# Norms of 512 tokens in a two-layer diffusion trunk: one tile of squares to sum in place of two, a chunk later, and the root's table loaded ahead

## What is computed

```python
def rmsnorm(x, w):
    xf = x.astype(jnp.float32)
    y = xf * lax.rsqrt(jnp.mean(xf * xf, axis=-1, keepdims=True) + EPS)
    return (y * w.astype(jnp.float32)).astype(x.dtype)

def modulate(h, shift, scale):
    return h * (1 + scale) + shift

x = x + 0.5 * mod[:, 2] * swiglu(modulate(rmsnorm(x, norm_w[0]), mod[:, 0], mod[:, 1]), ffn1_wi, ffn1_wo)
h = modulate(rmsnorm(x, norm_w[1]), mod[:, 3], mod[:, 4])
```

## Time and profile before

| | us |
|---|---|
| three runs | 1838.77, 1846.31, 1848.38; median 1846.31 |
| profiled execution, its own time | 1840.37 |
| its span, first to last instruction | 1838.2 |
| TensorE matmuls busy | 1821.0 |
| VectorE busy | 1120.6 |
| ScalarE busy | 694.2 |
| GpSimd busy | 99.3 |

### The profile page before, as it was taken

One profiled execution on the slowest core, in us unless ns is written; L12 is line 12 of the kernel. 1 busy time (PEld: TensorE's weight loads), 2 busy tenths in 40 slices (PEclk: granted clock), 3 DMA queues, 4 the chain that ended last, 5 costly groups with the idle time before them and its releaser, 6 DMA issues.

```text
span 1838.2 us, 26302 instructions
## 1 busy us (share of the span) xinstructions
PE 1821.0 (99%) x10125; PEld 1545.6 (84%) x10125; DVE 1120.6 (61%) x1506; ACT 694.2 (38%) x1093; POOL 99.3 (5%) x174
## 2 busy tenths in 40 slices
PE   8999999999999999999999999999999999999998
PEld 6788888888777789888888888888888889999998
DVE  5777736656554366877737558777322487676554
ACT  3433332144334324433332144333322365556553
POOL 0110001010000001000001010000000100000000
PEclk9999999999999999999999999999999999999999
DMA  9666526433222223666526435665232344446653
GB/s 335 216 186 189 159 99 224 146 77 93 80 81 69 88 84 127 183 189 190 159 92 229 148 115 172 180 196 162 92 103 91 73 146 138 149 147 197 194 195 114
DMA packets 187893, 271.49 MB, mean 148 GB/s; under 512 B 25388, under 2 KB 154908, under 8 KB 187804
## 3 DMA queue, kind: packets, MB, share of 16 engines
q1 hardware_dynamic: 168912, 202.74, 35.2%
q0 software_dynamic: 18432, 67.12, 11.8%
q10 hardware_dynamic: 460, 0.39, 0.1%
HBM read 269.16 MB, written 1.05 MB: 147 GB/s over the span
## 4 chain that ended last, share of the span: by engine, by line
PE 94%; DVE 2%; ACT 2%; issue 1%; DMA 0%; POOL 0%; SPq 0%; ACTq 0%; DVEq 0%
PE ps L573 23%; PE ps L574 23%; PE ps L575 23%; PE turned L573 2%; PE turned L575 2%; PE turned L574 2%; PE scored L573 2%; PE scored L575 2%; PE scored L574 2%; PE ps L630 2%; PE ps L632 2%; PE ps L642 2%; PE turned L943 1%; PE scored L912 1%; PE turned L926 1%; PE scored L604 1%
## 5 line engine op out<-in xcount | busy, mean ns | idle before, releaser
L1338 DVE TENSOR_TENSOR wL<-raw,wH 128x1024 fp32r<-128x1024 f32 x364 | 443.3, 1222 | 448.3 <-ACT wH L1054 448.0
L573 PE MATMUL ps<-hH,wH 128*128 128x512 f32 (+1 forms) x1832 | 652.8, 356 | 2.0 <-ACT T L1166 1.4
L574 PE MATMUL ps<-hL,wH 128*128 128x512 f32 (+1 forms) x1832 | 646.3, 353 | 0.0
L575 PE MATMUL ps<-hH,wL 128*128 128x512 f32 (+1 forms) x1832 | 646.1, 353 | 0.0
L1054 ACT ACTIVATE wH<-raw 128x1024 fp32r<-128x1024 f32 x364 | 383.3, 1057 | 667.2 <-PE ps L575 662.2
L573 PEld LDWEIGHTS ps<-hH,wH 128*128 128x128 f32 x1832 | 344.8, 188 | 69.8 <-issue 21.4
L575 PEld LDWEIGHTS ps<-hH,wL 128*128 128x128 f32 x1832 | 344.8, 188 | 48.2
L574 PEld LDWEIGHTS ps<-hL,wH 128*128 128x128 f32 x1832 | 344.9, 188 | 46.6
L573 PE MATMUL ps<-GH,wH 128*128 (+2 forms) x376 | 131.5, 350 | 0.0
L575 PE MATMUL ps<-GH,wL 128*128 (+2 forms) x376 | 131.2, 349 | 0.0
L574 PE MATMUL ps<-GL,wH 128*128 (+2 forms) x376 | 131.2, 349 | 0.0
(11 more groups left out here) (235 smaller groups left out, 2152.5 us busy)
## 6 DMA issues: line engine op xcount, KB each, us to landing
raw<-in_ffn_wi SPq DMA_DIRECT2D x176, 512.0 KB, 3.7
raw<-in_ffn_wo SPq DMA_DIRECT2D x88, 512.0 KB, 3.3
raw<-in_w_in SPq DMA_DIRECT2D x60, 512.0 KB, 3.9
adaC<-in_w_ada POOLq DMA_DIRECT2D x48, 512.0 KB, 4.5
adaW<-in_w_ada POOLq DMA_DIRECT2D x32, 512.0 KB, 4.6
adaA<-in_w_ada POOLq DMA_DIRECT2D x24, 512.0 KB, 4.0
adaB<-in_w_ada POOLq DMA_DIRECT2D x24, 512.0 KB, 4.6
raw<-in_w_out SPq DMA_DIRECT2D x16, 512.0 KB, 3.3
```

Source lines behind the costliest of these rows:

```text
L573: mm(dst, wa, ra, start=start, stop=False, **kw)
L574: mm(dst, wa, rb, start=False, stop=False, **kw)
L575: return mm(dst, wb, ra, start=False, stop=stop, **kw)
L1338: tt(wL[:, s, :], raw[:, s, :], wH[:, s, :].bitcast(F32), ALU.subtract).then_inc(lo_done, 1)
```

## The change

In the norms v = 1 to 4, GpSimd gets a fifth add for each half, of the tile with squares 6+7 into the tile with all the others, behind VectorE's add of 6+7. TensorE sums that one tile. The first half's sum moves from behind chunk 2 to behind chunk 3 and its spread from behind chunk 5 to behind chunk 6; the second half's from within chunk 1 to within chunk 2 and from within chunk 2 to within chunk 3. ScalarE's small activation that asks for the root's table stands ahead of the squares in norms 1 to 4 too.

```diff
-            return (0, 6) if beneath(v) else (0, 4, 6)
+            return (0,) if beneath(v) else (0, 4, 6)
...
-            each = [2 if q == 0 else 4 if beneath(q) else 3 for q in range(v + 1)]
+            each = [2 if q == 0 else 5 if beneath(q) else 3 for q in range(v + 1)]
...
-                    for i, (m, k) in enumerate(((0, 1), (2, 3), (0, 2)) + (((0, 4),) if beneath(v) else ())):
+                    for i, (m, k) in enumerate(((0, 1), (2, 3), (0, 2)) + (((0, 4), (0, 6)) if beneath(v) else ())):
...
-                            pool.wait_ge(sq_four, four_count(v, hf) + 3)
-                            pool.wait_ge(sq_pair, 2 * q + 1)
+                            pool.wait_ge(sq_four, four_count(v, hf) + i)
+                            pool.wait_ge(sq_pair, 2 * q + i - 2)
...
-                        if hf == 1 and at == 2:
+                        if hf == 1 and at == 3:
                             mean_squares(v, 0)
-                        if hf == 1 and at == 5:
+                        if hf == 1 and at == 6:
                             spread_roots(v, 0)
...
-                        pe.wait_ge(sq_four, four_count(v, hf) + (4 if beneath(v) else 3))
+                        pe.wait_ge(sq_four, four_count(v, hf) + (5 if beneath(v) else 3))
...
-                                  start=(m == 0 and tb == 0), stop=(m == 6), skip_group_check=True)
+                                  start=(m == 0 and tb == 0), stop=(m == sum_tiles(v)[-1]), skip_group_check=True)
...
-                return {(0, 1, "within"): lambda: mean_squares(v, 1), (0, 2, "within"): lambda: spread_roots(v, 1)}
+                return {(0, 2, "within"): lambda: mean_squares(v, 1), (0, 3, "within"): lambda: spread_roots(v, 1)}
...
                 if v > 0:
-                    if nh == 1:
-                        av(stat[:, 0, 0:1], epsT[:], ACT.Sqrt)
+                    av(stat[:, 0, 0:1], epsT[:], ACT.Sqrt)
```

## The result

| | before | after |
|---|---|---|
| median of 12 runs, us | 1838.65 | 1844.73 |
| lowest and highest | 1836.69, 1848.38 | 1842.92, 1853.31 |
| profiled execution, its span | 1838.2 | 1842.5 |

The ratio is 1.0031, with a 95% interval of 1.0021 to 1.0042: the change costs about 5.7 us, with bounds of 3.9 and 7.7. The forecast of the cost was +5.2 us. The forecast time of 1848.5 was 3.8 us too high, and the measured one lies in the range. All runs here are compared with runs of the kernel before on the same chip: e1 to e4 ran on one chip, e5 to e8 on another.

A forecast was written before the change was run, and what follows sets the result against it. TensorE, busy 1821.0 of 1838.2 us, was taken as the bound. Norms 1 to 4 cost 1.1 + 1.5 + 1.1 + 1.5 = +5.2 us, put on the mean 1843.5 for a forecast of 1848.5, range 1841 to 1856.

The forecast's parts named there:

- The prize: TensorE, norms 1 to 4: one tile less per sum saves 2.9 us, the first spread's lost wait 0.8; 3.7 in all.
- The table: ScalarE, norms 1 to 4: the root's 1.28 us table load, put ahead of the squares, falls in idle time, costing nothing.
- Rival C: At the root: the table does not last, a second 1.28 us load follows; +1 to +6 us on the forecast, chance 0.03.
- The sum of the first half: Norm 1: TensorE, ready at 398.65, waits 0.18 us for GpSimd's added add; the sum starts at 398.83.
- The first half's chain: Norm 1, spread to hH to opening: spread 0.33 us later, TensorE waits 0.68, opening at 403.43, 0.27 later than before.
- The second half: Norm 1: waits of 0.45 and 0.7 us for low parts of chunks 1 and 3; VectorE's diagonal 1.53 us later.
- Norms 2 and 4: VectorE's 1.53 us delay comes through whole, by the wait for hH in norm 2 and VectorE's list in 4; +1.5 each.
- norms 1 and 3: The wait for chunk 3's low part costs +1.1 us each; the modulation's sums that follow cover the rest.
- Rivals A and B: Norms 1 to 4: A, new waits all covered, -3.7 us, chance 0.12; B, clock halves, +15 us, chance 0.08.
- rival B: Norms 1 to 4: new waits let TensorE's clock fall to half, as after norm 5; +15 us or 1859, chance 0.08.

The follow-up runs named there:

- e1: Kernel before with only the root's table loaded ahead of the squares in norms 1 to 4: 1.22 us less over the norms, ratio 1.0002.
- e4: Changed kernel with the first half's spread back behind chunk 5 instead of 6: +2.74 us over norms 1 to 4 against before, ratio 1.0054.
- e5: Changed kernel with VectorE's low parts of weight piece and chunk 3 ahead of the second half's inverse root: +2.88 us over norms 1 to 4, ratio 1.0014.
- e8: Kernel before with twelve filling matmuls instead of six behind the spread of norm 5: ratio 0.9994, -0.01 us over norms 1 to 4.
- e3: Kernel before with the table ahead and the late sum and spread places, two tiles summed, no fifth add: +7.51 us over the norms, ratio 1.0055.
- e6: Changed kernel with both VectorE's list reordered and the first half's spread back behind chunk 5: +0.05 us over norms 1 to 4, ratio 0.9996.
- e7: Kernel before with the table ahead and VectorE's low part of the fourth weight piece one step later: -1.99 us over the norms, ratio 0.9977.
- e2: Changed kernel with sums and spreads back in their old places; one tile, fifth add and table ahead stay: +3.51 us over the norms, ratio 1.0028.

## Why the prediction was right

**The prize.** Right: 16 matmuls less (32 records), and the first spread's wait of 0.21 was gone, by the table (e1). The price of a tile was taken too low. I took the 0.36 between the starts of the two tiles. Where nothing waits, the matmuls on the two sides of the sum are 0.93 apart before (405.44 to 406.37) and 0.49 after, so a tile is worth 0.44; in the first half the wait for GpSimd eats it (see e3).

**The table.** Right: six loads ahead, none at the root's line, the load hidden in ScalarE's idle time. Rival C is out.

**The sum of the first half.** Predicted for norm 1 at 398.83 with a wait of 0.18; measured 399.00 with 0.19 (all measured times of this section are moved by the 1.72). TensorE was ready at 398.65, as predicted, so the wait recorded as 0.19 moved the sum by 0.35.

**The first half's chain.** Spread predicted at 401.52 and measured at 401.68, hH 402.77 and 402.84, opening 403.43 and 403.49, waiting 0.50 by the record and 0.68 by the sum.

**The second half.** hL matmuls of chunk 1 at 406.28 and 406.33, the sum at 407.72 and 407.86, the diagonal at 408.85 and 408.92, the hL matmuls of chunk 3 at 410.92 and 410.98. That what is queued behind the inverse root on VectorE carries the cost is shown by e5. The waits of L642 are recorded as 0.22 and 0.64; by the distances from start to start they cost 0.48 and 0.73, against the 0.45 and 0.7 of the sum.

**Norms 2 and 4.** Both wait at the second half's first matmul, and norm 4's two old waits are as long as before (0.69 and 1.26), since VectorE's whole list is late. They cost +1.56 and +1.58 against +1.5 each. The prediction says that norm 2 waits at this matmul in the kernel before already. The list of waits has none there, and the timeline leaves some 0.1 us for one: the four hL matmuls ahead take 0.59 from start to start (729.10 to 729.69), where those at 404.12 took 0.48.

```profile
729.10 0.64 PE L642 MATMUL ps<-hL,wH 128*128 128x256 f32 x4
729.69 0.35 PE L630 MATMUL ps<-hH,wH 128*128 128x256 f32 x1
```

**What was off.** Each of norms 1 and 3 was taken 0.15 too cheap and the total by 0.45 us. Of each 0.15, 0.1 is this: four hL matmuls that start from a wait cost 0.67 us (409.26 to 409.93), where I took their start alone to move; without a wait the same step took 0.57 (409.83 to 410.40). The level was off by 3.8 us. I put the 5.2 on the mean of four times (1843.5), which makes 1848.7 and not the 1848.5 written, but the median of before over 12 runs is 1838.65: two of the four times were of the upper group described below. The sum against the profiled execution's own 1840.37 gives 1845.6, within 0.9 us of the median measured. That the ratio of the runs gives 5.7 us, so near to the 5.65 of the traces, is partly luck: its interval is 3.9 to 7.7.

**Rivals A and B.** No chain was quicker than read. The granted clock was 1.00 in norm 1 (395 to 415 us) and in norm 4 (1462 to 1482), with TensorE busy for 18.5 and 16.4 of 20 us: waits of this size did not lower it. The row that rival B rests on does not show what the prediction says of it. From 1646.50 to 1648.00 TensorE is busy all the time, with filling matmuls of 128 columns. The 2-column matmuls and the waits lie ahead, from 1641.66 to 1644.67, and the clock fell there (it is 0.72 of full speed from 1643 to 1644 and 0.50 from 1644 to 1650). Nor does this stage always lower it. Here are the same 6.4 us around the spread of norm 5, first of before, then of e1: equally busy, once at half the clock and once at the full one.

```profile
1643.60:1650.00 6.40, 5.33 (x23) 0.50 0.28 86
```

```profile
1640.73:1647.13 6.40, 5.33 (x43) 1.00 0.28 86
```

## What to carry to other kernels

Before a step is moved later in one engine's list to hide a wait, follow the chain behind it: here the wait for GpSimd went from 0.9 us to 0.2 or nothing, and in norms 1 and 3 waits of 0.50, 0.22 and 0.64 us came back further on. A wait of an in-order engine delays all that is queued behind it, so work that is ready belongs ahead of it (e5 won 2.8 us with three lines in another order). And an edit of a tenth of a percent is read from the distance between two marks in the traces, which repeated within 0.04 us here, not from the whole time.

## What the runs showed of the hardware

**Two paces of the same matmuls at full clock.** Behind norm 5, from 1660 to 1820 us, TensorE works on matmuls of 256 columns, with one pause of 0.6 us. Two profiled executions, first of before, then of e4 (length, TensorE's busy time and matmuls, granted clock, DMA share, GB/s):

```profile
1660.00:1820.00 160.00, 159.38 (x1406) 1.00 0.59 190
```

```profile
1660.00:1820.00 160.00, 159.39 (x1355) 1.00 0.60 188
```

One does 1406 matmuls, the other 1355: 0.1133 against 0.1177 us from start to start, steady over the whole stretch. From the pause to the sum of norm 6 it is 166.86 us in before and 173.16 in e4:

```profile
1663.61 0.38 PE L573 MATMUL ps<-hH,wH 128*128 128x256 f32 x1 [0.62 <-ACT T L1147]
...
1830.47 0.58 PE L754 MATMUL scored<-cst,T 128*128 128x2 f32 x4 [0.23 <-DVE X L1424]
```

```profile
1666.02 0.38 PE L573 MATMUL ps<-hH,wH 128*128 128x256 f32 x1 [0.61 <-ACT T L1146]
...
1839.18 0.58 PE L754 MATMUL scored<-cst,T 128*128 128x2 f32 x4
```

The ten profiled executions have only these two lengths: 166.83 to 166.86 us in six, 173.16 to 173.17 in four, 6.3 us apart. Before, after, e1, e3, e6 and e7 ran it at the faster pace in their profiled execution, e2, e4, e5 and e8 at the slower. In e6 the 0.1177 shows earlier, from 1618 us to the end of the output projection, and is gone behind norm 5. It fits the two groups in the times of one kernel: of before, 17 of 25 runs beside e1 to e4 lie at 1836.7 to 1840.1 and the others at 1842.9 to 1846.0, and on the other chip, beside e5 to e8, 4 of 30 below 1838 and all others above 1842.9. Only one execution of each kernel has a trace, so that the two paces make the two groups is likely and not shown. What sets the pace stays open. All five runs of e4 were in the upper group (the slowest, 1851.41, at a mean granted clock of 0.946 where the others have 0.996), while a third of before's were, so it may hang on the kernel; e8 neither showed nor excluded that. These 6.3 us are more than the whole change costs.

**GpSimd and VectorE.** GpSimd's fifth add takes 0.74 us in the first half and 0.85 in the second, where the others into the same tile take 0.74 (timeline of GpSimd, norm 1 after):

```profile
396.40 0.74 POOL L548 TENSOR_TENSOR T<-T,sqT 128x256 f32<-128x256 f32 x1 [0.42 <-DVE sqT L1400]
...
403.13 0.74 POOL L548 TENSOR_TENSOR T<-T,sqT 128x256 f32<-128x256 f32 x1 [2.73 <-DVE sqT L1400]
404.30 0.85 POOL L548 TENSOR_TENSOR T<-T,sqT 128x256 f32<-128x256 f32 x1 [0.42 <-DVE sqT L1400]
```

The slower one starts at 404.30, while VectorE's low part of chunk 1 runs (from 404.08 for 0.47, two tensors in SBUF as inputs). Beside the one at 396.40 VectorE adds to the stream X, with one input in SBUF and one in PSUM. The lock of the Trainium skill (SBUF — State Buffer, § SBUF: two separate sides) would hold for the first pair and not for the second, and the trace agrees, for a second kind of VectorE instruction. The add became 0.11 us longer, less than the 0.25 for which VectorE's instruction still ran.
